# One-core hybrid decoder trunk: pooling, attention with gates between the heads, then state space in all four stages; mixer scratch laid out anew; last norm in three parts

## The reference, cut to what matters

```python
D_MODEL = 1024; BATCH = 1; SEQ = 512; DEPTH = 2           # all float32
POOL_WINDOWS = (2, 4, 8, 16)
PEER_HEADS = 8; PEER_TOPK = 16; PEER_NKEYS = 128           # 16384 experts

def reference(x, positions, ...):
    for l in range(DEPTH):
        h = rmsnorm(x, norm1_g[l])
        z = h @ w_in[l]
        u_pool, u_ssm, q, k, v, gate_logits = jnp.split(z, offsets, axis=-1)
        y_pool = pool_branch(u_pool, ...) @ pool_proj[l]
        y_ssm = ssm_branch(u_ssm, ...) @ ssm_proj[l]
        y_attn = attention_branch(q, k, v, positions) @ attn_proj[l]
        g = jax.nn.sigmoid(gate_logits).reshape(B, L, N_BRANCHES, D)
        merged = g[:, :, 0] * y_pool + g[:, :, 1] * y_ssm + g[:, :, 2] * y_attn
        x = x + merged @ w_out[l]
        h2 = rmsnorm(x, norm2_g[l])
        x = x + peer_ffn(h2, ...)      # per token and head: 16 experts picked, their rows gathered
    return rmsnorm(x, final_g)

def peer_ffn(...):                     # e: 128 picks a token, g: their softmax
    a = jnp.einsum('cd,ckd->ck', hx, u_tab[e])
    return jnp.einsum('ck,ckd->cd', g * jax.nn.gelu(a), v_tab[e])
```

## Time and profile before

| | |
|---|---|
| median of 3 runs | 3755.12 us (3745.66 to 3757.23) |
| profiled execution | 3761.48 us, its span 3759.7 us |
| instructions | 37763 |
| PE busy | 86% of the span |
| DVE busy | 67% |
| POOL busy | 62% |
| ACT busy | 25% |
| moved by DMA | 1305.56 MB, mean 347 GB/s |

### The profile page before, as it was taken

How to read it: one execution, slowest core, us unless ns; L and a number is a source line. 1 busy time by engine, 2 the same in 40 slices (tenths; PEclk the granted TensorE clock), 3 DMA queues, 4 the chain that set the end, 5 groups by cost and what they waited for, 6 DMA issues and landing times.

```text
span 3759.7 us, 37763 instructions
## 1 busy us (share of the span) xinstructions
PE 3216.2 (86%) x11496; PEld 2073.9 (55%) x11496; DVE 2533.9 (67%) x6139; ACT 950.8 (25%) x2095; POOL 2342.0 (62%) x2114
## 2 busy tenths in 40 slices
PE   8989899878988999867988999877988986777776
PEld 7778656445765656544765656544765642232233
DVE  6465788867566888766566888766566888444443
ACT  2331233323111243312111243323111222111111
POOL 1000476767667776666666776767666777777773
PEclk9989999989999999878999999989998988888888
DMA  5255799999999999999999999999999999999995
GB/s 176 90 202 202 289 381 386 380 356 357 401 386 384 385 382 381 377 347 338 395 387 384 395 385 379 374 342 355 395 400 372 390 340 349 362 373 369 365 365 216
DMA packets 361577, 1305.56 MB, mean 347 GB/s; under 512 B 40417, under 2 KB 42849, under 8 KB 361121
## 3 DMA queue, kind: packets, MB, share of 16 engines
q0 software_dynamic: 298960, 1087.79, 76.1%
q1 hardware_dynamic: 62416, 215.35, 15.1%
HBM read 1288.30 MB, written 14.68 MB: 347 GB/s over the span
## 4 chain that ended last, share of the span: by engine, by line
PE 36%; POOL 25%; DMA 17%; issue 12%; DVE 9%; another core or an unknown queue 1%; ACT 0%; DVEq 0%; SPq 0%; ACTq 0%; POOLq 0%
POOL heap L897 25%; DMA heap<-table_u,heap 17%; PE ps L1147 14%; PE ps L939 14%; DVE heap L2080 2%; PE ps L989 2%; DVE heap L1782 2%; PE ps L1084 1%; PE ps L1068 1%; PE ps L1034 1%; PE ps L1046 0%; PE ps L1028 0%; PE ps L970 0%; DMA ring<-ssm_par 0%
## 5 line engine op out<-in xcount | busy, mean ns | idle before, releaser
L1147 PE MATMUL ps<-heap 128*128 128x512 f32 x3268 | 1652.4, 645 | 352.3 <-ACT heap L1399 238.6
L2080 DVE CUSTOM_DVE_ANT_0 heap<-heap 128x1024 f32<-128x1024 f32 x1024 | 1251.5, 1222 | 946.6 <-DMA heap<-table_u,heap 879.6
L897 POOL DMA_INDIRECT heap<-table_v,heap x1024 | 1187.5, 1160 | 691.2 <-issue 265.2
L897 POOL DMA_INDIRECT heap<-table_u,heap x1024 | 1120.0, 1094 | 364.6 <-issue 312.1
L1147 PEld LDWEIGHTS ps<-heap 128*128 128x128 f32 x3268 | 653.7, 206 | 1046.6 <-issue 734.1
L939 PE MATMUL ps<-hT,ring 128*128 128x256 f32 x3840 | 895.6, 383 | 14.7 <-DVE hT L1902 9.8
L939 PEld LDWEIGHTS ps<-hT,ring 128*128 128x128 f32 x3840 | 735.1, 192 | 230.5 <-issue 133.3
L1399 ACT ACTIVATE heap<-ident,heap 128x128 f32<-128x128 f32 x817 | 292.4, 392 | 523.2 <-DVE heap L2091 275.2
L1782 DVE SCALAR_TENSOR_TENSOR heap<-heap 128x1024 f32<-128x1024 f32 x201 | 257.7, 1282 | 10.5 <-DVE stats L1949 4.5
L1419 ACT ACTIVATE heap<-heap 128x8 f32<-128x8 f32 x128 | 26.7, 208 | 941.2 <-DVE heap L2080 751.8
L1084 PE MATMUL ps<-temp,ring 128*128 128x256 f32 x640 | 151.7, 385 | 9.2 <-DVEq L1996 4.2
(11 more groups left out here) (255 smaller groups left out, 2588.5 us busy)
## 6 DMA issues: line engine op xcount, KB each, us to landing
ring<-weights SPq DMA_DIRECT2D x344, 512.0 KB
ring<-ssm_par SPq DMA_DIRECT2D x48, 512.0 KB
heap<-table_u,heap POOLq DMA_INDIRECT x1024
heap<-table_v,heap POOLq DMA_INDIRECT x1024
ssm_par<-heap POOLq DMA_DIRECT2D x20, 512.0 KB, 6.2
ring<-weights SPq DMA_DIRECT2D x20, 256.0 KB
xT<-x_cm SPq DMA_DIRECT2D x2, 1024.0 KB, 9.6
ssm_par<-heap POOLq DMA_DIRECT2D x8, 256.0 KB, 2.8
```

Of the source, the lines that this page charges most:

```text
L897: pool.indirect_dma_start(rows[:, j, :], None, table, bass.IndirectOffsetOnAxis(expert[:, tile % 2, k:k + 1], 0)).then_inc(landed, 16)
L1147: mm = pe.matmul(ps[:, 4 + 2 * (tile % 2) + half, :], diag[:, PE_TURN[v] % DIAGS, :], rows_v[:, v % NV, half * 512:(half + 1) * 512], star ...
L2080: dve.tensor_tensor_reduce(row, row, h_tok[:, tile % 2, :], 1.0, 0.0, ALU.mult, ALU.add, act_st[:, g % 3, pick % GROUP:pick % GROUP + 1]). ...
```

## The change

`first_order` and `merge_order` are gone. One `stage_order(u)` writes all four stages: norm, pooling, q, k, v, attention with the four pool pairs between the first heads and `ssm_u` at the later ones, then `ssm_x`, `ssm_y` and the GLU with the attention gates between them, then the state-space gates, `out`, norm and search. In stage 0 `ssm_x` 0 and 1 move from the last head to behind it. The mixers' tiles get one layout for all stages, and four waits on the stage before are gone. The last norm becomes three planned steps, `final` 0 (tiles 4 and 5, 256 tokens), 1 (tile 6) and 2 (tile 7, 128 tokens each), each put into the plan when its tiles are home. The last 24 sums may go to DVE too.

```diff
-def first_order():
+def stage_order(u):
...
+    out = [("squares", u, 0), ("mean", u, 0), ("pool_u", u, 0)] + ([] if u else [("angles", 0)])
+    out += [("pool_u", u, 1), ("windows", u)] + prep(0) + ([("inject", u)] if u % 2 else [])
+    out += [(kind, u, i) for kind in ("q", "k") for i in range(3)] + ([] if u else [("masks", 0)]) + [("v", u, 0)]
...
+    fill = [[("v", u, 1), ("v", u, 2)], [("mix", u, 0), ("mix", u, 1)] + pair(0, 0), pair(1, 0), pair(2, 0), pair(3, 0)]
+    if u == 0:
+        fill += [[("ssm_u", u, 0), ("ssm_u", u, 1)], weigh(0)[:8], weigh(0)[8:10]]
+    else:
+        fill += [[("ssm_u", u, 0)], [("ssm_u", u, 1)], []]
+    out += attention_order(u, att, fill) + prep(1)
+    out += [("ssm_x", u, 0), ("ssm_x", u, 1)] + pair(0, 2) + [("ssm_y", u, 0), ("ssm_x", u, 2), ("ssm_x", u, 3)]
+    out += ([] if u else weigh(0)[10:]) + pair(1, 2) + [("ssm_y", u, 1)] + pair(2, 2)
+    out += [(kind, u, i) for i in range(2) for kind in ("glu_gate", "glu_val")] + pair(3, 2)
     for mm in range(4):
         out += pair(mm, 1)
...
-def stage_order(u):
-    out = [("squares", u, 0), ("mean", u, 0), ("ssm_u", u, 0), ("ssm_u", u, 1)]
-    out += [("inject", u)] if u % 2 else []
-    out += [(kind, u, i) for kind in ("q", "k", "v") for i in range(3)]
-    att = [(2 * (u % 2) + T, h) for T in range(2) for h in range(SLOTS)]
-    fill = [[("ssm_x", u, 0), ("ssm_x", u, 1)], [("ssm_y", u, 0)], [("ssm_x", u, 2), ("ssm_x", u, 3)], [("ssm_y", u, 1)],
-            [("pool_u", u, 0), ("pool_u", u, 1), ("windows", u)], [("glu_gate", u, 0), ("glu_val", u, 0)],
-            [("glu_gate", u, 1), ("glu_val", u, 1)], [("mix", u, 0), ("mix", u, 1)]]
-    return out + attention_order(u, att, fill) + merge_order(u) + query_order(u)
...
+FINALS = ((TILES - 3, 0, N), (TILES - 2, N, P), (TILES - 1, N + P, P))
...
-            slot["v_on"] = "DVE" if v % PICKS % 2 == 1 and v % PICKS < PICKS - 1 and not queue["TOP"] and at < len(order) and (v < PICKS or ready([(("drain", v // PICKS - 1), 1)], s)) else "PE"
+            slot["v_on"] = "DVE" if v % PICKS % 2 == 1 and v % PICKS < PICKS - 1 and not queue["TOP"] and (at < len(order) or v >= TILES * PICKS - 24) and (v < PICKS or ready([(("drain", v // PICKS - 1), 1)], s)) else "PE"
...
+        while finals and ready([(("drain", FINALS[finals[0]][0]), 2)] + prior(("final", finals[0])), s):
+            enqueue(("final", finals.popleft()), 0, s)
...
-            for half in range(2):
-                sp.wait_ge(final_ready, half + 1)
-                sp.dma_start(out_cm[:, half, :].rearrange("p (k t) -> p k t", t=N), hT[:]).then_inc(out_stored, 16)
+            for n, (_, t0, width) in enumerate(FINALS):
+                sp.wait_ge(final_ready, n + 1)
+                sp.dma_start(out_cm[:, t0 // N, :].rearrange("p (k t) -> p k t", t=N)[:, :, t0 % N:t0 % N + width],
+                             hT[:, :, t0 % N:t0 % N + width]).then_inc(out_stored, 16)
...
-                    if u and i == 0:
-                        act.wait_ge(tiles_done, UNIT[("mix", u - 1, 1)] + 1)
...
-                    if u and i == 0:
-                        act.wait_ge(gate_used, LAST_GATE[u - 1] + 1)
...
-                if u:
-                    dve.wait_ge(tiles_done, UNIT[("out", u - 1, 0)] + 1)
...
-                    if kind == "q" and i == 0 and u:
-                        dve.wait_ge(tiles_done, UNIT[("score", u - 1, PH - 1)] + 1)
```

More of the change, by code:

```diff
@@ L105, in first_order @@
     for mm in range(4):
         out += pair(mm, 1)
-    return out + weigh(1) + [("out", 0, i) for i in range(4)] + [("mean", 0, 1)] + query_order(0)
+    return out + ([] if u else weigh(1)) + [("out", u, i) for i in range(4)] + [("mean", u, 1)] + query_order(u)
 def attention_order(u, att, fill):
@@ L113, in attention_order @@
         out += [("att_s", u, T, h, g) for g in range(3)] + [("att_e", u, T, h)]
-        out.append(fill[n][0])
+        out += fill[n][:1]
         if n:
@@ L119, in attention_order @@
     return out + [("att_o", u) + att[-1]]
-def merge_order(u):
-    out = []
-    for mm in range(4):
-        for b in range(3):
-            out += [("branch", u, mm, b), ("gate", u, mm, b)]
-    return out + [("out", u, i) for i in range(4)] + [("mean", u, 1)]
 def query_order(u):
@@ L209, in prior @@
         return [end("drain", 2 * u - 4 + i) for i in range(2)] if u >= 2 else []
+    if kind == "final":
+        return [end("htok", STAGES - 1, 1, 1)] + ([end("final", u - 1)] if u else [])
     if kind == "mean":
@@ L275, in whole_order @@
 def whole_order():
-    out = first_order()
-    for u in range(1, STAGES):
-        out += stage_order(u)
-    return out
+    return [item for u in range(STAGES) for item in stage_order(u)]
 ORDER = whole_order()
@@ L955, in emit @@
                     return
+                if kind == "final":
+                    t0, width = FINALS[u][1] % N, FINALS[u][2]
+                    pe.wait_ge(bank_free[u], BANK_TOTAL[u])
+                    pe.wait_ge(squares_done, 4 * (2 * STAGES + u + 1))
+                    for k in range(KD):
+                        mm = pe.matmul(ps[:, u, 0:width], mean_ones[:], hT[:, k, t0:t0 + width], start=(k == 0), stop=(k == KD - 1))
+                        if k == KD - 1:
+                            mm.then_inc(final_mean, 1)
+                        yield
+                    return
                 b = unit(item)
@@ L1164, in run_pe @@
             assert not live
-            for half in range(2):
-                pe.wait_ge(squares_done, 4 * (2 * STAGES + half + 1))
-                for k in range(KD):
-                    mm = pe.matmul(ps[:, half, 0:N], mean_ones[:], hT[:, k, :], start=(k == 0), stop=(k == KD - 1))
-                mm.then_inc(tiles_done, 1)
         def run_act(act):
@@ L1195, in emit @@
                     yield from squares(u, norm_of(u, 0))
+                elif kind == "final":
+                    tile, t0, width = FINALS[u]
+                    if part == 0:
+                        act.wait_ge(x_home, 2 * (tile + 1))
+                        if u == 0:
+                            act.wait_ge(tiles_done, len(RING_UNITS))
+                        else:
+                            act.wait_ge(out_stored, 16 * u)
+                        for i in range(4):
+                            act.activation(hT[:, 2 * i:2 * i + 2, t0 % N:t0 % N + width], xT[:, 2 * i:2 * i + 2, t0:t0 + width],
+                                           ACT.Square).then_inc(squares_done, 1)
+                            yield
+                    else:
+                        act.wait_ge(final_mean, u + 1)
+                        act.wait_ge(normed, 9 * (2 * STAGES + u))
+                        act.activation(rms[:, 0:width], ps[:, u, 0:width], ACT.Sqrt, bias=eps[:, 0:1]).then_inc(root_done, 1)
+                        yield
                 elif kind == "mean":
```

137 lines of the change are left out of this document (57 added, 80 removed).

## The result

The changed kernel takes **3807.36 us** (median of 4 runs, 3800.49 to 3808.92), the kernel before in the same comparison 3756.18 us (3745.66 to 3761.63): a ratio of 1.0142, with an interval of 1.0125 to 1.0158. It is slower by some 51 us, where 3735 was forecast and 3770 was the upper end of the range.

| | before | after | difference |
|---|---|---|---|
| up to the end of the first dot | 410.9 | 420.9 | +10.0 |
| first dot to last dot | 3293.7 | 3351.6 | +57.9 |
| last dot to the end | 55.1 | 33.4 | -21.7 |

A forecast was written before the change was run, and what follows sets the result against it. Bounds: DMA transfers in the stream, PE in stage 0, a chain through all engines at the end. Terms: -25.5 + 10 + 3 + 2 - 10 = -20.5 us, giving 3741 profiled, 3735 median; 8-in-10 range 3706 to 3770.

The forecast's parts named there:

- Term 1: The end: last sums shared by DVE and PE and a shorter last norm and store, -25.5 us.
- Term 2: Stage 0: `ssm_y` starts later, after idle PE and then at a lower clock, delaying the first gather, +10 us.
- Terms 3 and 4: Output stores between picks in the stream, +3 us; POOL waiting for first picks of tiles 2 and 6, +2 us.
- Term 5: The stream: attention regains part of its idle DMA share, less a cost at the spins, net -10 us.
- I count 1 to 2 us a stage: Stream: cost of spins standing in slots where PE has little and only DVE works, 1 to 2 us a stage.
- both should give back a third to a half: Attention: moving `windows` out and pool gates in recovers a third to a half of lost DMA share, 11 to 17 us.
- The spins' stretch starves the gathers: Rival, chance 0.14: in 38 slots a stage DVE's dots, sums and spins slow the gathers, net +40 us; 3785.
- Bytes are the bound: Rival, chance 0.25: attention's gathers reach at most 360 GB/s, term 5 is 0, store paid in full; -9.5 us, 3746.
- Attention fills up: Rival, chance 0.15: attention runs at 385 GB/s like the q, k, v stretch, 34 us come back; 3711.
- the end does not shrink: Rival, chance 0.03: at the end DVE sums wait for landings in order and hold up dots; 3755.

The follow-up runs named there:

- experiment 4: Kernel before with only the change's end: last norm in three planned parts, last 24 v sums allowed on DVE; 3732.10 us, ratio 0.9965.
- experiment 1: Changed kernel with state-space tables `tab0` and `tab1` loaded into the unused half of `kT` instead of the ring; 3754.03 us, ratio 1.0018.
- (5): Changed kernel with tables outside the ring and two branch-and-gate pairs, not one, between `ssm_x` and `ssm_y` in all stages; 3737.61 us, ratio 0.9979.
- experiment 3: Changed kernel with `ssm_y` of stages 1 to 3 planned at least six slots after its last spin instead of one; 3799.54 us, ratio 1.0137.

## Why the prediction was wrong, step by step

**Term 1, the end, -25.5: right, 4 us too large.** (Its own parts, 8.7 and 29.2 - 12.4, make 25.5; the 25.3 beside it is a slip.) From the last dot to the end it is 33.4 us, where 30 was forecast. The end of after, all engines:

```profile
3784.42 1.28 DVE L1779 SCALAR_TENSOR_TENSOR heap<-heap 128x1024 f32<-128x1024 f32 x1 [2.67 <-DMA heap<-table_v,heap]
...
3786.29 3.67 PE L1148 MATMUL ps<-heap 128*128 128x512 f32 x8 [1.86 <-DMA heap<-table_v,heap]
...
3793.79 1.33 ACT L1201 ACTIVATE hT<-xT 128x256 f32<-128x256 f32 x4 [13.76 <-DVE xT L2065]
...
3795.27 3.40 PE L952 MATMUL ps<-hT,mean_ones 128*128 128x128 f32 x16 [2.83 <-ACT hT L1201]
...
3800.10 2.19 DVE L1898 SCALAR_TENSOR_TENSOR hT<-xT,fing,rms 128x128 f32<-128x128 f32 x8
3802.38 0.38 SPq L793 DMA_DIRECT2D out_cm<-hT  x1
```

From the squares to the end of the scalings it is 8.5 us (8.2 forecast), the store 3.6 (4.2 forecast). The size that was off is that of the sums: they end at 3789.96, 17.4 us behind the last dot instead of 13.4. Both engines wait there for v rows, 2.67 and 1.86 us in these lines: the gathers' landing sets the pace, not the sums, and dividing the sums between two engines shortens only what is not landing.

**Term 2, stage 0, +10: right in each step.** PE's timeline and POOL's:

```profile
226.10 0.66 PE L1013 MATMUL ps<-temp,ring 128*128 128x64 f32 x2 [12.16 <-DMA ring<-ssm_par]
```

```profile
415.28 1.04 POOL L888 DMA_INDIRECT heap<-table_u,heap  x1 [52.09 <-DVE heap L1888]
```

`ssm_y` at 226.1 (227 forecast), 12.2 us idle before it (some 10), records of 0.63 us at the lower clock up to 236, the first gather at 415.28 (415). The size has a scatter, though: the first dot ends at 410.9, 413.4, 414.8, 415.3 and 417.2 us in the five kernels with the old stage 0, and at 420.9, 424.4 and 419.8 in those with the new one and its ring; the means differ by 7.4.

**Terms 3 and 4, +3 and +2.** The two short waits of POOL for first picks did not come: after has one wait on L1888, 52.1 us, that of the first tile, so term 4 is 0. The stores can't be told from the noise: the kernel of experiment 4 pays them too and has no longer a stream than before (3290.4 against 3293.7).

**Term 5, the stream, -10: wrong, and nearly the whole miss.** Terms 3 to 5 were to give -5; the stream is 57.9 us longer, 63 of the 67 us by which the profiled execution misses the forecast. Two steps of it failed.

The step "I count 1 to 2 us a stage", for the spins with little of PE's work beside them, is 79 us in three stages, 26 us a stage. The cost was mis-sized because a wait was missing from it. The prediction looked at the rate at a spin and at DVE's load, and never followed the pieces of the ring in stages 1 to 3. It had done just that for stage 0 in term 2: the second spin frees a slot, the loads start, 7.7 us later PE starts. The same order of steps, the same ring and the same three pieces between table and `ca0` stand in each of the other stages, twice. Six waits could have been forecast, which the trace now shows with 12 to 22 us each; at term 2's own 10 us they would have given +60 and a time near 3795. Stage 0 had even less at stake, since nothing but the trunk stood behind PE; in the stream the sums, the v buffers and all gathers do.

The step "both should give back a third to a half" failed as well. Half of its reason came true: with the pool gates between the heads the granted clock in attention is 0.95, 0.91 and 0.94 instead of 0.89, 0.82 and 0.87. The rate did not follow: 360, 365 and 365 GB/s instead of 364, 355 and 358, not 370 to 385. A slot in attention takes 3.31 us in either kernel (841 us for 254 slots, 751 for 227). So PE's clock did not set the rate there. What does is open; I made no run that takes attention apart. The 358 GB/s of the Trainium skill are no answer: the Trainium skill, Perfetto Trace Analysis, Engine Utilization, says that this figure is the share of a core whose neighbour is active too, and that a core by itself can draw about 120% of it, an estimate of 430. The rows agree that more is to be had: 400 GB/s over 174 us.

**The rivals.** *The spins' stretch starves the gathers* (0.14, 3785) was the case in sign, place and threshold: 4.00 us a slot over its 38 slots, against the 3.65 that it named. Its mechanism was wrong. It wanted DVE full; DVE was busy 111 of 178 us, and in experiment 1, with the same spins on DVE, three fifths of the three pieces' loss are gone (30 us left of 79). With its real cause it costs more, and attention returned none of the 25 us: hence 3807 and not 3785, beyond the range. *Bytes are the bound* was right on term 5's own ground, attention gained nothing, but could not see the loss. *Attention fills up* and *the end does not shrink* are out (365 GB/s; 33.4 us).

The four waits removed and the new layout were put at nothing, and nothing in the traces speaks against it: with the waits of `ssm_y` gone (5) no loss is left for them.

## What to carry to other kernels

When steps are moved, write down the sequence of the pieces of every shared ring, count back by its size from each piece, and ask who frees that slot and when: a slot that is freed by the consumer of the result for which the next piece is needed makes a chain of wait, load and start, and it is paid at every place where the order repeats. A wait that was found and priced in one stage must be looked for in every other stage with the same order, and there priced by what stands behind it in the queue of the engine: here waits of 12 and 7 us in a stage without gathers came with a first dot 7 to 10 us later, and waits of 12 to 22 us in the stream cost 13 us each and stopped POOL and DVE with PE. Against such a wait helps work of other kinds in between, or a place of its own for what is held long; a hole in the plan cost about as much here as the wait (ratio 1.0137 in experiment 3, 1.0142 in the change).
